# The delta rule stage: order of masks, gated convolutions, state products and splits

## What is computed

```python
decay = exp(where(causal, g[..., :, None] - g[..., None, :], -inf))
lower = where(strict, (k_beta @ k.T) * decay, 0)
u, w  = triangular_solve(lower + eye, [v_beta, k_beta * exp(g)])
qk    = (q @ k.T) * decay
# scan over the 4 chunks, S starts at 0
v_new = u_i - w_i @ S
o_i   = q_dec_i @ S + qk_i @ v_new
S     = S * g_last + k_dec_i.T @ v_new
```

## Time and profile before

| | us |
|---|---|
| median of three runs | 3767.84 |
| profiled execution, its own time | 3761.1 |
| its span | 3759.3 |
| PE busy | 3588.2 (95%) |
| DVE busy | 1981.8 (53%) |
| ACT busy | 1221.3 (32%) |
| delta stage, layer 0 | 2433.0 to 2620.0 |
| delta stage, layer 1 | 3148.7 to 3336.3 |

### The profile page before, as it was taken

The page is one execution under the profiler, slowest core; times in us unless marked ns, Lnnn a source line. Parts: engine busy times, 40 slices in busy tenths (PEclk is TensorE's granted clock), DMA queues, the critical chain, the costliest instruction groups (busy, mean ns, idle before and its releaser), DMA issues. The chain is left out here.

```text
span 3759.3 us, 43412 instructions
## 1 busy us (share of the span) xinstructions
PE 3588.2 (95%) x17810; PEld 2961.3 (79%) x17810; DVE 1981.8 (53%) x3051; ACT 1221.3 (32%) x1916; POOL 149.1 (4%) x212
## 2 busy tenths in 40 slices
PE   6999999999999999999999998998999999989999
PEld 4888778678887888777678886787788878877887
DVE  5655566665456645566664355665322366553233
ACT  2223324532233222333532223634222354442222
POOL 1110100001000100100000001000000000000000
PEclk8999999999999999999999999999999999999999
DMA  6664321145443644321143331211233222113332
GB/s 238 227 198 135 78 86 46 51 143 187 140 140 102 222 159 135 96 68 46 51 129 116 111 132 46 79 34 51 79 101 123 96 48 72 40 51 98 93 107 79
DMA packets 438042, 397.75 MB, mean 106 GB/s; under 512 B 53779, under 2 KB 390275, under 8 KB 437844
## 3 DMA queue, kind: packets, MB, share of 16 engines
q1 hardware_dynamic: 413028, 310.53, 27.0%
q0 software_dynamic: 24816, 84.45, 6.6%
HBM read 390.14 MB, written 4.78 MB: 105 GB/s over the span
## 5 line engine op out<-in xcount | busy, mean ns | idle before, releaser
L163 PE MATMUL m_ps<-m_h_high,ffn_w_high 128*128 128x512 f32 x2100 | 823.8, 392 | 0.0
L164 PE MATMUL m_ps<-m_h_low,ffn_w_high 128*128 128x512 f32 x2100 | 819.3, 390 | 0.0
L165 PE MATMUL m_ps<-m_h_high,ffn_w_low 128*128 128x512 f32 x2100 | 819.2, 390 | 0.0
L165 PEld LDWEIGHTS m_ps<-m_h_high,ffn_w_low 128*128 128x128 f32 x2100 | 395.5, 188 | 83.4
L163 PEld LDWEIGHTS m_ps<-m_h_high,ffn_w_high 128*128 128x128 f32 x2100 | 396.2, 189 | 82.4
L164 PEld LDWEIGHTS m_ps<-m_h_low,ffn_w_high 128*128 128x128 f32 x2100 | 396.0, 189 | 81.6
L953 ACT ACTIVATE ffn_sil<-m_ps 128x512 f32<-128x512 f32 x132 | 79.1, 599 | 1139.0 <-PE m_ps L165 1139.0
L163 PE MATMUL m_ps<-ffn_w_high,ffn_hid_high 128*128 128x512 f32 x1056 | 412.3, 390 | 0.0
L165 PE MATMUL m_ps<-ffn_w_high,ffn_hid_low 128*128 128x512 f32 x1056 | 411.7, 390 | 0.0
L164 PE MATMUL m_ps<-ffn_w_low,ffn_hid_high 128*128 128x512 f32 x1056 | 411.4, 390 | 0.0
L993 DVE TENSOR_TENSOR ffn_hid<-ffn_sil,m_ps 128x512 f32<-128x512 f32 x110 | 75.6, 687 | 560.4 <-ACT ffn_sil L953 560.4
(11 more groups left out here) (470 smaller groups left out, 5564.1 us busy)
## 6 DMA issues: line engine op xcount, KB each, us to landing
m_raw<-in_ffn_w SPq DMA_DIRECT2D x176, 512.0 KB, 4.7
ffn_rows<-in_ada_w POOLq DMA_DIRECT2D x128, 512.0 KB, 5.0
ffn_rows<-in_ffn_w SPq DMA_DIRECT2D x88, 512.0 KB, 3.4
m_raw<-in_w_in SPq DMA_DIRECT2D x32, 1024.0 KB, 5.5
m_raw<-in_ffn_w_gate SPq DMA_DIRECT2D x44, 512.0 KB, 3.7
m_raw<-in_ffn_w_up SPq DMA_DIRECT2D x44, 512.0 KB, 4.8
ffn_rows<-in_ffn_w_down SPq DMA_DIRECT2D x44, 512.0 KB, 3.2
m_raw<-in_w_out SPq DMA_DIRECT2D x24, 512.0 KB, 4.4
```

What stands on the lines that cost most here:

```text
L163: pe.matmul(out, sh, mh, start=first, stop=False, skip_group_check=True)
L164: pe.matmul(out, sh, ml, start=False, stop=False, skip_group_check=True)
L165: return pe.matmul(out, sl, mh, start=False, stop=last, skip_group_check=True)
```

## The change

It moves work within the queues of one stage, and changes what some of it waits for; the only instruction kinds added are waits, and one signal, `state_read`.

- **Preparation.** In the last tile DVE makes masks 0 and 1 (with Y 0 and Y 1) right after the product with qk, ahead of the q scaling, kbg, kdec and vb. PE waits for all of the preparation (`prep_free`) ahead of the first product of unit 2 instead of unit 0.
- **Convolutions.** `gated_convolution(n, half)` is no longer part of `evacuate`. Half 0 (the product and the first tap) comes at the end of DVE's odd units 1, 7, 15 and 23, half 1 (two taps and the last product) at the end of units 2, 8, 16 and 24. ACT's square is a step of its own, `square(n)`, at the end of its units 4, 10, 18 and 26.
- **Scan.** Tile 0 waits for two u copies (and for three w copies ahead of its output product), and writes k x v_new to bank 4. In the other tiles the four q x S products run together ahead of the wait for v_new and signal `state_read`; DVE decays the state after that signal instead of after `o`, and gates output i - 1 after the state instead of before it.
- **Splits.** The casts of the gated part on ACT lie between the w copies; the low parts on DVE lie between the u copies, the last one in tile 0 of the scan.

```diff
--- before.py
+++ after.py
@@ -2447,7 +2447,7 @@
...
                "lt_ready qk_ready k_turned v_turned nat_ready masked t1 t1_copied x_up xy_ready y_turned x_copied u_ready w_ready u_copied w_copied "
-               "ws v_new o o_squared o_copied o_normed s_add s_ready root_ready prep_free mix_turned mix_high mix_ready sc_high "
+               "ws state_read v_new o o_squared o_copied o_normed s_add s_ready root_ready prep_free mix_turned mix_high mix_ready sc_high "
                "w_high w_split product act_evacuated dve_evacuated gated squared sc_root sc_scaled pad gate_chain", mine) as (block, S):
@@ -2536,6 +2536,8 @@
...
                 pe.wait_ge(S.masked, u + 1)
+                if u == 2:
+                    pe.wait_ge(S.prep_free, TT)
                 if u >= 3:
@@ -2565,7 +2567,6 @@
...
 
-            pe.wait_ge(S.prep_free, TT)
             for u in range(UNITS + 1):
@@ -2598,26 +2599,31 @@
...
 
-            pe.wait_ge(S.u_copied, TT)
-            pe.wait_ge(S.w_copied, TT)
             for i in range(TT):
+                pe.wait_ge(S.u_copied, TT if i else 2)
+                if i:
+                    pe.wait_ge(S.w_copied, TT)
+                out = M.ps[:, 1 + i % 2]
                 if i:
...
                     mm.then_inc(S.ws, 1)
+                    if i >= 2:
+                        pe.wait_ge(S.o_copied, i - 1)
+                    for h in range(DH):
+                        mm = pe.matmul(head(out, h), tok(q, h, i), head(A.state, h), start=(h == 0), stop=False, skip_group_check=True)
+                    mm.then_inc(S.state_read, 1)
                     pe.wait_ge(S.v_new, i)
-                if i >= 2:
-                    pe.wait_ge(S.o_copied, i - 1)
                 vn = A.v_new if i else A.u[:, 0]
...
                     for h in range(DH):
-                        mm = pe.matmul(head(M.ps[:, 3], h), head(A.kdec[:, i], h), head(vn, h), start=True, stop=True)
+                        mm = pe.matmul(head(M.ps[:, 3 if i else 4], h), head(A.kdec[:, i], h), head(vn, h), start=True, stop=True)
                     mm.then_inc(S.s_add, 1)
+                if i == 0:
+                    pe.wait_ge(S.w_copied, 3)
                 for h in range(DH):
-                    if i:
-                        pe.matmul(head(M.ps[:, 1 + i % 2], h), tok(q, h, i), head(A.state, h), start=True, stop=False)
-                    mm = pe.matmul(head(M.ps[:, 1 + i % 2], h), head(A.qk[:, i], h), head(vn, h), start=(i == 0), stop=True)
+                    mm = pe.matmul(head(out, h), head(A.qk[:, i], h), head(vn, h), start=(i == 0), stop=True, skip_group_check=True)
                 mm.then_inc(S.o, 1)
@@ -2647,13 +2653,22 @@
...
                     high(e + 2)
-                before = sequence[n - 1] if n else GATED
-                if before < GATED and before % 3 == 2:
-                    c = before // 3
-                    act.wait_ge(S.gated, c + 1)
-                    if c:
-                        act.wait_ge(S.product, place[GATED + c - 1] + 1)
-                    act.activation(A.sq[:], A.scT[:, c, :], ACT.Square).then_inc(S.squared, 1)
+
+            def square(n):
+                e = sequence[n]
+                if e >= GATED or e % 3 < 2:
+                    return
+                c = e // 3
+                act.wait_ge(S.gated, c + 1)
+                if c:
+                    act.wait_ge(S.product, place[GATED + c - 1] + 1)
+                act.activation(A.sq[:], A.scT[:, c, :], ACT.Square).then_inc(S.squared, 1)
+
+            def high_gated(c):
+                act.wait_ge(S.sc_scaled, c + 1)
+                if c == 0:
+                    act.wait_ge(S.product, place[GATED - 1] + 1)
+                act.copy(M.h_high[:, DH + c, :], A.scT[:, c, :]).then_inc(S.sc_high, 1)
 
@@ -2684,13 +2699,13 @@
...
                     evacuate(4 + (u - 3) // 2)
+                if u >= 4 and u % 2 == 0 and 2 + (u - 4) // 2 < len(sequence) - 1:
+                    square(2 + (u - 4) // 2)
             evacuate(len(sequence) - 1)
...
                 act.copy(A.wT[:, i], M.ps[:, first_bank(UNITS + i) + 1]).then_inc(S.w_copied, 1)
-            for c in range(SCT):
-                act.wait_ge(S.sc_scaled, c + 1)
-                act.copy(M.h_high[:, DH + c, :], A.scT[:, c, :]).then_inc(S.sc_high, 1)
+                high_gated(i)
 
@@ -2716,12 +2731,18 @@
...
 
-            def gated_convolution(c):
-                for e in range(3 * c, 3 * c + 3):
-                    dve.wait_ge(done(e), evacuated(e))
+            def gated_convolution(n, half):
+                e = sequence[n]
+                if e >= GATED or e % 3 < 2:
+                    return
+                c = e // 3
                 x, y = A.prod[:, c % 2, :], A.gate_c[:, c % 2, :]
-                gate_link(dve.tensor_tensor(x[:, SCCONV - 1:], x[:, SCCONV - 1:], y, ALU.mult))
-                gate_link(dve.tensor_scalar(y, x[:, 0:T], A.sc_w[:, 0, c:c + 1], None, ALU.mult))
+                if half == 0:
+                    for part in range(3 * c, 3 * c + 3):
+                        dve.wait_ge(done(part), evacuated(part))
+                    gate_link(dve.tensor_tensor(x[:, SCCONV - 1:], x[:, SCCONV - 1:], y, ALU.mult))
+                    gate_link(dve.tensor_scalar(y, x[:, 0:T], A.sc_w[:, 0, c:c + 1], None, ALU.mult))
+                    return
                 for j in range(1, SCCONV):
@@ -2742,8 +2763,21 @@
...
                     low(e + 2)
-                if e % 3 == 2:
-                    gated_convolution(e // 3)
+
+            eye = M.ident[:].unsqueeze(1).to_broadcast([P, DH, P])
+
+            def mask(u):
+                n, i = u // TT, u % TT
+                if n:
+                    dve.wait_ge(S.t1, u - TT + 1)
+                else:
+                    dve.wait_ge(S.lt_ready, i + 1)
+                    dve.wait_ge(S.qk_ready, i + 1)
+                dve.tensor_tensor(heads(A.BT[:, i]), heads(A.LT[:, i]), M.levels[:, n, :].unsqueeze(1).to_broadcast([P, DH, P]),
+                                  ALU.mult).then_inc(S.masked, 1)
+                if n == 0:
+                    dve.wait_ge(S.masked, u + 1)
+                    link(dve.tensor_tensor(heads(Y[:, i]), eye, heads(A.BT[:, i]), ALU.subtract))
 
@@ -2769,6 +2803,10 @@
...
                 dve.tensor_tensor(A.qk[:, i], M.ps[:, 3], D, ALU.mult).then_inc(S.qk_ready, 1)
+                if i == TT - 1:
+                    dve.wait_ge(S.v_turned, TT)
+                    for u in range(2):
+                        mask(u)
                 dve.tensor_tensor(q[:, :, i * P:(i + 1) * P], q[:, :, i * P:(i + 1) * P], heads(A.rows[:]), ALU.mult
@@ -2777,20 +2815,6 @@
...
                 dve.tensor_tensor(heads(A.vb[:, i]), heads(M.ps[:, 5]), cols(beta_all, i), ALU.mult).then_inc(S.prep_free, 1)
-            dve.wait_ge(S.prep_free, TT)
-            dve.wait_ge(S.lt_ready, TT)
...
             def update(u):
@@ -2802,19 +2826,29 @@
...
 
-            mask(0)
-            mask(1)
             evacuate(TT - 1)
...
                 update(u)
-                if u >= 3 and u % 2 and 4 + (u - 3) // 2 < len(sequence) - 1:
-                    evacuate(4 + (u - 3) // 2)
+                n = 4 + (u - 3) // 2
+                if u >= 3 and u % 2 and n < len(sequence) - 1:
+                    evacuate(n)
+                if u >= 1 and u % 2 and 2 <= n - 1 < len(sequence) - 1:
+                    gated_convolution(n - 1, 0)
+                if u >= 2 and u % 2 == 0 and 2 <= n - 1 < len(sequence) - 1:
+                    gated_convolution(n - 1, 1)
             evacuate(len(sequence) - 1)
+
+            def low_gated(c):
+                dve.wait_ge(S.sc_high, c + 1)
+                low_part(dve, M.h_low[:, DH + c, :], A.scT[:, c, :], M.h_high[:, DH + c, :])
+
             for i in range(TT):
...
                 dve.tensor_copy(A.u[:, i], M.ps[:, first_bank(UNITS + i)]).then_inc(S.u_copied, 1)
+                if i:
+                    low_gated(i - 1)
 
@@ -2829,26 +2863,25 @@
...
 
-            def low_gated(c):
-                dve.wait_ge(S.sc_high, c + 1)
-                low_part(dve, M.h_low[:, DH + c, :], A.scT[:, c, :], M.h_high[:, DH + c, :])
-
             state, vn = heads(A.state[:]), A.v_new[:]
...
                     dve.tensor_tensor(vn, A.u[:, i], M.ps[:, 0], ALU.subtract).then_inc(S.v_new, 1)
-                    gate_output(i - 1)
                 if i < TT - 1:
-                    dve.wait_ge(S.s_add, i + 1)
                     if i:
-                        dve.wait_ge(S.o, i + 1)
+                        dve.wait_ge(S.state_read, i)
                         dve.wait_ge(S.s_ready, i)
                         link(dve.tensor_tensor(state, state, cols(A.gain[:, 32:48], i), ALU.mult))
+                        dve.wait_ge(S.s_add, i + 1)
                         dve.tensor_tensor(A.state[:], A.state[:], M.ps[:, 3], ALU.add).then_inc(S.s_ready, 1)
                     else:
```

(8 more changed lines are left out.)

10 lines of the change are left out of this document (removed).

## The result

The kernel after the change takes 3754.84 us (median of 18 runs, 3749.71 to 3759.57), the kernel before 3766.2 us beside it (median of 18, 3757.78 to 3770.17). The ratio is 0.9975, with a 95% interval of 0.9968 to 0.9982: faster, by 0.25%. I had forecast 3755.4 and a range of 3746 to 3764. The profiled execution took 3749.71 us, with a span of 3747.9 for 3759.3.

A forecast was written before the change was run, and what follows sets the result against it. PE, busy 95% of the span, bounds the kernel, so only its idle or slow-clocked time counts. Per layer 5.5 - 2.3 - 0.5 + 3.3 = 6.0, taken as 6.2; 3767.84 - 12.4 = 3755.4 us, range 3746 to 3764.

The forecast's parts named there:

- Step 1: End of preparation, first units: masks 0 and 1 ahead, first convolution moved out; 5.5 us a layer won.
- Step 2: Units 8 and 16: second convolution halves delay masks and the next dense tiles; 1.17 us lost at each.
- Step 3: Units 22 to 27, last convolution: 4.9 us won are spent again, 0; booked -0.5 a layer for the clock.
- the term for the clock: Units 22 to 27: clock falling in the 2.2 us gap costs 0.9 more; booked as -0.5 a layer.
- Step 4: Scan: earlier start 0.93, two tiles at 5.72 for 6.45, last tile 0.9; sum 3.3 us a layer won.
- list of idle times: PE idle 20.2 us in the first stretch: 4.2 and 3.3 at the inverse, 9.3 scan, 2.4 dense tiles, 0.9 scan start.
- A: Whole stage: output turn does not hold PE, halves vanish in idle time; 34.8 us won, 3733; chance 0.06.
- B: Convolution halves: each second half costs its full 2.19, last convolution loses 2; 4.8 us won, 3763; chance 0.14.
- C: Scan: 1.56 us wait brings 1.2 GHz for three tiles, 12 us a layer; 11.6 slower, 3779; chance 0.03.

The follow-up runs named there:

- e1: Kernel after with masks and convolutions put back, leaving only the new scan and splits: 3759.6 us for 3763.97, ratio 0.999.
- e4: Kernel after with the second convolution halves of units 8 and 16 ahead of the update instead of behind it: 3749.47 us, ratio 0.9964.
- e5: Kernel after with PE's turn of each output moved one tile later, behind the next tile's q x S: 3746.82 us for 3762.7, ratio 0.9958.
- e6: Kernel after with the last two Ln, then the two Exp, grouped behind ACT's unit loop: 3748.23 us, ratio 0.9961.
- e10: Kernel after, unchanged, executed once more for a second profile: 3746.74 us, one execution of before beside it 3759.25.
- e7: Kernel after with second halves ahead of updates, output turns one tile later and Ln/Exp grouped: 3735.42 us for 3762.7, ratio 0.9927.
- e3: Kernel before with only the convolutions in halves between units and ACT's squares moved: 3761.49 us, ratio 0.9997.
- e9: The kernel before with only convolution halves and squares moved, executed a second time for a profile: 3764.53 us, before beside it 3759.25.

## Why the prediction was right, and where it was not

**Step 1**, forecast 5.5 us a layer, measured 5.63 and 6.17. Right, term by term: the waits for masks 0 and 1 are gone, mask 3 costs 0.30 (forecast 0.57), the square of block 0 costs 0.57 (forecast 0.6). Layer 1's 0.54 more is before's own: it stood at 65.17 there for 64.62, and in e1, with the same code, at 64.02, so that a gain read against one execution is good to about 0.6 us here. The two edits share a wait: alone the masks win 2.83 and the halves 4.41 in layer 0, 7.24 in sum, together 5.63. An account edit by edit that is not made on one common clock would have booked the 1.6 us twice.

**Step 2**, forecast 1.17 lost at each of two places, 2.34 a layer, measured 2.30 and 2.29; e4, which takes the halves from behind the update, gives back 2.28 and 2.30. Right in size. The place is a little other than I had it: I looked for it in the waits of dense tiles, which would grow from 2.4 to 4.7; they stay at 2.2, and the other 2.4 us are the two waits of 1.2 for masks 11 and 19 ahead of the first products behind which these tiles stand. The sum, 4.6, is the same, since mask and split stand in one queue behind the half.

**Step 3**, forecast 0, less 0.5 for the clock, measured 0.26 and 0.25 won. Where the clock did not fall, the waits came as worked out (layer 1 of e4: 2.16 for the copy, 0.81 for mask 26, 1.51 for mask 27; forecast 2.2, 0.6 and 1.6). In after it did fall behind the 2.16 us wait (0.60 and 0.72 in the windows above), and the waits for masks 26 and 27 are 0.75 and 0.34 in layer 0, and none and 0.71 in layer 1. The step that failed is the term for the clock. That it would fall, the rows had left open; the Trainium skill (TensorE: Matmul & The Clock Gate, HAM oscillation) warns of it for waits between groups of products, and the windows of after agree. But I was wrong to charge for it: what the slow products took longer, the waits for masks 26 and 27 became shorter. The two layers of e4 show it in one kernel, with the six us behind the wait of 2.16 at 0.72 in layer 0 and at 1.00 in layer 1:

```profile
2577.27:2583.27 6.00, 5.48 (x32) 5.29 (x33) 5.86 (x10) 2.72 (x5) 0.00 (x0) 0.72 0.01 3
...
3284.98:3290.98 6.00, 4.10 (x32) 3.68 (x33) 5.86 (x10) 2.72 (x5) 0.00 (x0) 1.00 0.00 0
```

From the last dense tile to the solutions they take 30.73 and 30.70 us. A fall is paid only where PE is on the path, and even here that holds only for as long as there is a wait left to shorten: in layer 0 of e5 the clock was at 0.50 up to 2585.00, past the place of the wait for mask 27, and 1.2 us were lost. Six profiled executions have this wait, twelve layers: the clock fell behind it in ten, and nine of the ten falls cost 0.15 us at most. The other 0.25 that was won is not the clock's, since e4 and e5 won it in layer 1 without a fall too (30.70 and 30.71 for 30.98); the forecast's sum for these units was 0.3 too long.

**Step 4**, forecast 3.3, measured 3.03 and 2.87 (e1 alone 3.03 and 3.23). In layer 0 the start of the scan gave 0.94 (forecast 0.93), the two tiles 0.70 each (0.73; 5.75 us apart for 5.72), the last tile 0.88 (0.89), and at the end about 0.2 went again. In layer 1 the first of the two tiles gave only 0.37: the gating's last step came 0.34 later behind its own reciprocal, and the turn waited 1.90 us for 1.56. It does so in layer 1 of e4, e6 and e10 as well; why, stays open. e5 settles that the turn's place in PE's queue held the pace: with it moved, the tiles are 4.01 and 4.30 apart.

**The sum.** The steps made 6.0 a layer (I took 6.2), the profile has 6.62 and 7.00: 0.1 and 0.7 too little at the front, 0.5 that I charged for the clock and 0.25 that I missed beside it, and 0.3 and 0.4 too much at the scan. The profiled span fell by 11.4 where I said 12.4. In the timed runs the ratio gives 9.4 us (6.8 to 12.1) and the two medians differ by 11.4, so the gain of 12.4 stands just above what was measured, and that the forecast time is within 1 us has luck in it: the three runs from which I started were 1.6 us above the median of 18, which made up for the gain that I took too large. That the runs give less than the stages' 13.6 can have to do with falls of the clock at chance places, as in e10, whose stages won only 12.4; which falls the timed runs had is not known. One sum of the forecast came out by chance: its list of idle times counts the 0.9 us at the scan's start twice, since the 25 us of the scan hold it, and leaves out the 0.97 before the second turn. Nothing else hangs on that list.

**The rivals.** A, all waits go: no; but much of it was there to be had, by moves that the change does not make: the halves (e4), the tables (e6) and the tiles of the scan (e5). e7 has all three, 27 us under before where A said 34.8. B, the halves cost more: no; the two behind the updates cost 1.15 each and not 2.19, and step 3 lost nothing. e3 alone shows no gain that can be told (0.9997), but by the clock in the scan and not by DVE's queue. C, the clock falls in the scan: the mechanism exists, at 1.4 to 1.7 us a time in e3 and e9 and not 12 a layer, less than half of the 4.0 us that one whole tile at 1.2 GHz would cost; in after it did not occur (1.00 from 2590 to 2606).

## What to carry to other kernels

When an in-order queue is relieved of work, write down what each engine does next on one clock and charge every edit against that; gains of two edits that shorten one wait don't add up, while gains in parts that follow each other did to 0.2 us. Work that is moved off a busy stretch should go into the mover's idle time and ahead of the step that ends it: the same 2.2 us cost 1.15 behind the update and nothing ahead of it. Once the chain is shortened, look in the queue for side work that is in front of the chain's next step: here a turn with 0.4 us of its own held back each state product by about 1.5.
